# The head norm of a gated linear attention: sums by one product with a block matrix of ones, roots by logarithm and exponential on ScalarE

## The reference

```python
def rmsnorm(x, g):
    xf = x.astype(jnp.float32)
    y = xf * lax.rsqrt(jnp.mean(xf * xf, axis=-1, keepdims=True) + EPS)
    return (y * g.astype(jnp.float32)).astype(x.dtype)

    o_b, new_gla = gla_recurrence(...)          # (B, L, 4 heads, 64)
    o_b = rmsnorm(o_b.astype(x.dtype), gla_g.reshape(GLA_HEADS, GLA_DV))
    b_out = o_b.reshape(B, L, GROUP_W) * jax.nn.silu(g_z)
```

## Time and profile before

| what | value |
|---|---|
| median of 3 runs | 2264.63 us (2263.82 to 2267.15) |
| profiled execution, first to last instruction | 2263.7 us |
| PE busy | 2224.6 us, 98% |
| PEld, DVE, ACT, POOL busy | 80%, 58%, 40%, 5% |
| TensorE clock granted | 0.999 |

### The profile page before, as it was taken

How to read it: one execution, slowest core, us unless ns; L and a number is a source line. 1 busy time by engine, 2 the same in 40 slices (tenths; PEclk the granted TensorE clock), 3 DMA queues, 4 the chain that set the end, 5 groups by cost and what they waited for, 6 DMA issues and landing times.

```text
span 2263.7 us, 39453 instructions
## 1 busy us (share of the span) xinstructions
PE 2224.6 (98%) x14668; PEld 1809.6 (80%) x14668; DVE 1309.4 (58%) x2870; ACT 897.3 (40%) x2015; POOL 105.2 (5%) x179
## 2 busy tenths in 40 slices
PE   8999999999999999999999999999999999999998
PEld 4778877788788888878877878777878888887877
DVE  4467655565376755646536776556645666654542
ACT  4444233353454333434425442244435542343321
POOL 1000000000000000000000000000000000000000
PEclk9999999999999999999999999999999999999999
DMA  7111212244211122324331121232441112241332
GB/s 250 32 57 29 57 38 66 66 147 139 85 39 30 43 64 74 72 77 137 132 89 44 29 52 43 52 96 78 141 135 42 44 30 64 48 103 38 97 110 75
DMA packets 230552, 172.08 MB, mean 76 GB/s; under 512 B 56886, under 2 KB 206908, under 8 KB 230332
## 3 DMA queue, kind: packets, MB, share of 16 engines
q1 hardware_dynamic: 226100, 154.78, 24.3%
q10 hardware_dynamic: 4264, 14.78, 1.9%
HBM read 136.60 MB, written 21.93 MB: 70 GB/s over the span
## 4 chain that ended last, share of the span: by engine, by line
PE 51%; DVE 1%; issue 1%; ACT 0%; DVEq 0%; ACTq 0%; POOLq 0%; POOL 0%
PE bank L1767 27%; PE bank L2814 13%; PE bank L1861 2%; PE bank L2071 1%; PE bank L2046 1%; PE bank L2022 1%; PE bank L2830 1%; PE bank L1839 1%; PE bank L2027 1%; PE bank L1845 1%; PE bank L1910 0%; PE bank L1814 0%; PE bank L1908 0%; PE bank L1934 0%; PE bank L1911 0%
## 5 line engine op out<-in xcount | busy, mean ns | idle before, releaser
L1767 PE MATMUL bank<-h_hi,w_hi 128*128 128x512 f32 (+3 forms) x2160 | 482.9, 361 | 15.1 <-issue 5.7
L1767 PE MATMUL bank<-h_lo,w_hi 128*128 128x512 f32 (+3 forms) x2160 | 484.6, 361 | 1.7
L1767 PE MATMUL bank<-h_hi,w_lo 128*128 128x512 f32 (+2 forms) x2080 | 462.5, 360 | 2.2
L1767 PEld LDWEIGHTS bank<-h_hi,w_hi 128*128 128x128 f32 (+1 forms) x2160 | 353.2, 186 | 90.7 <-issue 32.7
L1767 PEld LDWEIGHTS bank<-h_lo,w_hi 128*128 128x128 f32 (+1 forms) x2160 | 352.3, 185 | 72.7 <-issue 15.1
L1767 PEld LDWEIGHTS bank<-h_hi,w_lo 128*128 128x128 f32 x2080 | 345.3, 188 | 64.7 <-issue 12.9
L2814 PE MATMUL bank<-scr_r,tb_r 128*128 128x512 f32 x816 | 195.1, 395 | 1.0 <-issue 1.0
L2814 PEld LDWEIGHTS bank<-scr_r,tb_r 128*128 128x128 f32 x816 | 151.7, 188 | 35.6 <-issue 2.3
L2139 ACT ACTIVATE tb<-bank 128x512 f32<-128x512 f32 (+1 forms) x140 | 71.5, 510 | 226.2 <-PE bank L1767 217.3
L2295 ACT ACTIVATE scr<-bank 128x1024 f32<-128x1024 f32 x64 | 65.8, 1027 | 194.9 <-PE bank L2046 194.9
L2814 PE MATMUL bank<-w_hi,tb_r 128*128 128x512 f32 x544 | 136.1, 394 | 0.0
(11 more groups left out here) (299 smaller groups left out, 2928.1 us busy)
## 6 DMA issues: line engine op xcount, KB each, us to landing
w_raw<-in_w_in SPq DMA_DIRECT2D x96, 512.0 KB, 3.8
out<-scr SPq DMA_DIRECT2D x32, 512.0 KB, 2.7
scr<-in_w_out SPq DMA_DIRECT2D x16, 512.0 KB, 5.3
w_raw<-in_w_out SPq DMA_DIRECT2D x16, 512.0 KB, 3.6
scr<-in_x_prompt SPq DMA_DIRECT2D x16, 512.0 KB, 3.7
scr<-out SPq DMA_DIRECT2D x16, 512.0 KB, 3.4
rot<-out ACTq DMA_DIRECT2D x12, 512.0 KB, 3.7
mix_t<-in_x_prompt ACTq DMA_DIRECT2D x8, 512.0 KB, 14.9
```

The source lines that it names most:

```text
L1767: m = mm(bank[b][0:m_w, 0:c1 - c0], w[:, slot, k, 0:m_w], h[:, k, c0:c1], start=it["piece"] == 0 and k == 0, stop=it["piece"] == 2 and k = ...
```

## The change

The squares now move through PE and a 128x128 block matrix of ones (`heads_one`, which has a one where row and column belong to the same head) stands as weights: one fp32 product of 128x512 puts the sum of each head on all 64 partitions of that head. So nothing has to be spread or turned. ACT takes the logarithm of the sum / 64 + EPS straight from bank 7, frees the bank, and takes exp(-0.5 x) in place; DVE multiplies from SBUF. `spread` is gone, and a part `root` on ACT (due when the sums are there) stands in its place; `gla_norm` no longer uses PE or bank 6, and POOL has no part in the norm.

```diff
@@ planner, Forecast.place
-            p = run("PE", 0.38 if small else 1.0, self.needs(it))
-            p = run("DVE", 0.2, p)
+            at[("full", n)] = run("PE", 0.14 if small else 0.86, self.needs(it))
+        elif k == "root":
+            p = self.table_run("ln", 0.25 if small else 0.65, when(("full", n)))
             self.free(p, 7)
-            at[("root", n)] = run("POOL", 0.8 if small else 1.7, p)
-        elif k == "spread":
-            at[("spread", n)] = run("DVE", 0.25 if small else 0.45, when(("root", n)))
+            at[("root", n)] = self.table_run("exp", 0.25 if small else 0.65, p)
         elif k == "gla_norm":
-            p = run("PE", 0.27 if small else 0.66, self.needs(it))
-            self.free(run("DVE", 0.3 if small else 0.78, p), 6)
-            run("DVE", 0.3 if small else 0.78)
+            run("DVE", 0.35 if small else 1.5, self.needs(it))
@@ TensorE
                     emptied(pe, it, 7)
-                    for c in range(n_ch):
-                        m = mm(bank[7][0:tw, 2 * c:2 * c + 2], sq[:, c * tw:(c + 1) * tw], heads_one[:, 0:P:HD],
-                               start=True, stop=True)
-                    m.then_inc(bank_full[7], 1)
-                elif kind == "gla_norm":
...
-                    for c in range(n_ch):
-                        m = nc.tensor.transpose(bank[6][:, c * tw:(c + 1) * tw],
-                                                qb_of(s)[0:tw, P * c:P * c + P], ident[0:tw, 0:tw])
-                    m.then_inc(bank_full[6], 1)
+                    mm(bank[7][:, 0:w], heads_one[:], sq, start=True, stop=True).then_inc(bank_full[7], 1)
@@ ScalarE
+                elif kind == "root":
...
+                    filled(act, it["of"], 7)
+                    link(fn(r, bank[7][:, 0:w], ACT.Ln, scale=1.0 / HD, bias=tiny[:]))
+                    act.drain().then_inc(bank_free[7], 1)
+                    fn(r, r, ACT.Exp, scale=-0.5).then_inc(rs_done, 1)
@@ VectorE
-                elif kind == "gla_sq":
...
-                    ts(z, bank[7][0:tw, 0:2 * n_ch], 1.0 / HD, EPS, ALU.mult, ALU.add).then_inc(ms_done, 1)
-                    dve.drain().then_inc(bank_free[7], 1)
-                elif kind == "spread":
...
-                    nc.vector.tensor_copy(qb_of(s)[0:tw].rearrange("p (x d) -> p x d", d=HD),
-                                          z.rearrange("p (x o) -> p x o", o=1).to_broadcast([tw, 2 * n_ch, HD])
-                                          ).then_inc(spread_done, 1)
                 elif kind == "gla_norm":
...
-                    filled(dve, it, 6)
-                    link(tt(r, bank[6][:, 0:w], area(lay, "o"), ALU.mult))
-                    dve.drain().then_inc(bank_free[6], 1)
+                    dve.wait_ge(rs_done, norm_no[s["n"]])
+                    link(tt(r, r, area(lay, "o"), ALU.mult))
@@ GpSimd
-                elif kind == "gla_sq":
...
-                    tt(z, z, minus_half[0:tw].to_broadcast([tw, n]), ALU.pow).then_inc(rs_done, 1)
```

More of the change, by code:

```diff
@@ L200, in needs @@
                  "gla_sq": [("sq", n), ("state", n, it.get("last", 0))],
-                 "gla_norm": [("spread", n)],
+                 "gla_norm": [("root", n)],
                  "score": [("turned", n), ("q", n), ("keyed", n), ("kct", n)],
@@ L523, in work @@
             out.append(item("gla_sq", [7], step=s, last=chunks - 1))
-            out.append(item("gla_norm", [6], step=s))
+            out.append(item("gla_norm", step=s))
         else:
@@ L597, in emit @@
         elif kind == "gla_norm":
-            while ("spread", n, 0) not in placed:
-                emit_part("spread")
+            while ("root", n, 0) not in placed:
+                emit_part("root")
         if kind == "gla_o":
@@ L623, in emit @@
         elif kind == "gla_sq":
-            parts.append((fc.at[("root", n)], "DVE", item("spread", step=it["step"], of=it)))
+            parts.append((fc.at[("full", n)], "ACT", item("root", step=it["step"], of=it)))
         elif kind == "evict" and it["role"] == "z":
@@ L736, in ready @@
         kind, n, c = it["kind"], it["step"]["n"] if "step" in it else 0, it.get("c", 0)
-        part = {"turn": ("scale", n, c), "fac_prod": ("fac_exp", n, it.get("i", 0)), "gla_norm": ("spread", n, 0)}.get(kind)
+        part = {"turn": ("scale", n, c), "fac_prod": ("fac_exp", n, it.get("i", 0)), "gla_norm": ("root", n, 0)}.get(kind)
         held = [float("inf") if behind_turn(x) else when + PART_US["held"] for when, _, x in parts if x["kind"] == "soft" and keeps_banks(x)
@@ L1162, in on_gpsimd @@
         def on_gpsimd(pool):
+            nc.gpsimd.memset(tiny[:], EPS)
             nc.gpsimd.memset(minus_half[:], -0.5).then_inc(out_sq_done, 1)
```

37 lines of the change are left out of this document (7 added, 30 removed).

## The result

The changed kernel takes 2307.61 us (median of 4 runs, 2300.63 to 2310.81) against 2264.99 of the kernel before beside it; ratio 1.0182, 95% interval 1.0165 to 1.0199. It is slower, as forecast, but by 43 us where I had written 14, and above the range of 2262 to 2297. The profiled execution is the fastest of the four: span 2298.8 us, 35.1 over the span before. Each timed run of this study lies 1.8 us above its span (2300.63 and 2298.8 here), not a tenth of a microsecond as I had concluded from the runs before; that moves the forecast by one microsecond and changes no reading.

The account below looks back on a forecast made before the run. It took the time to be the sum of what PE issues, the order hiding nearly all else. Waits grow by 30 us, PE work falls by 16: net +14 on 2263.7, so 2278 us, 8-in-10 range 2262 to 2297.

Parts of the forecast that it names:

- What PE saves: PE, norm product, transposes and turns: 12 us in prompt steps, 2 in sample steps, 2 in turns; 16 us (10 to 20).
- the turns and the sample steps: PE: fewer turns away from projections save 2 us (0 to 4), the four sample steps 2 us (0 to 3).
- Rival D: ACT's roots: no loads between Ln and Exp, so no waits at the ends of B; about 2255 us, chance 0.02.
- The block of 3.8 us: ACT, end of each B step: one root as two table loads, a logarithm and an exponential, 3.8 us together.
- Place by place: Second pass: PE waits of 2.5, 2.5, 1.5, 0.7 at B group ends, 8.6 in unit C; less today's 1.9, 13.9.
- PE's busy time: A sign of the forecast over the whole kernel: PE busy lower by some 15 us.
- place 5: Unit C, group 1, second half: no projections between, so the softmax chain sets the pace; PE waits 8.6 us (4 to 11).
- A: Rival: ACT reaches the roots earlier, waits are absorbed and grow by 6 against 16 saved; 2254 to 2255 us, chance 0.12.
- B: Rival: waits at the B ends at half, place 5 at 5.5, cancelling the saving; about 2265 us, chance 0.10.
- place 1: End of B group 0, first half, second pass: the root delays ACT's eviction, so PE waits 2.5 us.
- C: Rival: delays spread from one B end to later slots, the B-end waits doubled, place 5 at 11; 2300 us, chance 0.10.
- place 2: End of B group 0, second half, second pass: PE waits 2.5 us for ACT's work and DVE's gate after it.

Follow-up runs that it names:

- e9_idle: The kernel before with one idle pause on TensorE ahead of each of the 16 prompt steps' norm products; 2362.26 us, ratio 1.0429.
- e10_filled: The kernel before with the same 16 waits as e9_idle, filled with three products whose results are thrown away; 2327.62 us, ratio 1.0275.
- e11_short: The kernel before with the pauses of e9_idle at half the length (GpSimd operation 128x6 in place of 128x16); 2313.41 us, ratio 1.0211.
- e2_noload: The changed kernel with Tanh in place of the logarithm, same order, 40 table loads fewer; 2293.93 us, ratio 1.0132.
- e3_oldorder: The changed kernel's operations with the planner's costs of the kernel before, so nearly the old order; 2275.81 us, ratio 1.0056.
- e12_rest: The changed kernel with one planner constant changed (REST_US 2.0 to 0.0), giving another order in the C slot; 2281.19 us, ratio 1.0061.
- e6_replanned: The changed kernel with all its loads under other planner costs, the root due 2 us after its product; 2256.76 us, ratio 0.9968.
- e16_e7noload: The change with Tanh for Ln in the control's order, a 128x8 product standing where the four transposes stood; 2250.84 us, ratio 0.9942.
- the control: The kernel before, without the change, under retuned planner constants (EARLY 0.4, REST_US and RETURN_US 0, soft 4.5); 2251.87 us, ratio 0.9940.

## Why the prediction was wrong in size

**The step that failed** is the sentence that the clock plays no part because it is granted in full in the kernel before. That was true of a kernel with hardly any wait over 1.3 us, and I then forecast some sixteen waits of 1 to 4.4 us and priced them at their length alone. In the profiled run the lower level cost up to 21 us more than before, in the median run about 30, where the forecast had nothing. e9_idle and e10_filled show the mechanism, e11_short that it reaches down to waits of 1.5 us in about half of the cases. With the price of e9_idle (2.3 for 3.1) on the forecast's waits of 2 us and more, 2.5 + 2.5 + 4.4 + 2.0 in each second pass, 2 x 11.4 x 0.74 = 17 more, the forecast would have been 2295, inside my range and still 13 under the median.

**What PE saves.** Forecast 16 us, measured 13.4. The new product costs 0.86 us in place of the 0.95 that I took, the lower bound: 0.46 from its start to the next projection, and the one behind that comes 0.40 late. Twenty of them:

```profile
L1926 PE MATMUL bank<-scr,heads_one 128*128 128x512 f32 x16 | 8.2, 592 | 0.0
L1926 PE MATMUL bank<-mix_t,heads_one 128*128 128x512 f32 x16 | 8.2, 591 | 0.0
...
L1926 PE MATMUL bank<-scr,heads_one 128*128 128x64 f32 x8 | 1.3, 245 | 0.0
```

So the 16 prompt steps gave 16 x (1.70 - 0.86) = 13.4 instead of 12. The whole rest of the span fell by no more than that, so the turns and the sample steps together gave nothing that this split shows, where I had put 4 on them.

**The loads.** 81 in the program where there were 41; the 40 more stand one ahead of each of the root's two activations:

```profile
L2218 ACT ACT_TABLE_LOAD x20 | 25.7, 1283 | 0.5
L2220 ACT ACT_TABLE_LOAD x20 | 25.7, 1283 | 2.1
```

Rival D is out. The block of 3.8 us is 3.9.

**The waits.** Forecast +30, measured +27.4. Place by place in the first of the second passes: 2.5, 2.5, 1.5, 0.7 and 8.6 were forecast, 2.3, 3.0, 1.8, none and 8.7 measured (0.7 of the last was there before). Each first pass has one of 2.1 where I had said 1; e2_noload keeps it, so the loads are not its cause. PE's busy time, which I expected to fall by 15, rose by 7, since products at half clock count longer: as a sign it needs the clock beside it. What I put down to order (place 5) was order: e3_oldorder, e12_rest and e6_replanned don't have it (the waits of the transposes are none over 0.7, 0.5 and at most 1.4 us there).

**The rivals.** A and B ask for smaller waits than the trace has: 2.33 us at place 1, where A has none, and 8.7 in the C slot, where A has 4 and B 5.5. C gave 2300 through delays that spread; the trace shows no such spread, its waits over 1 us are those of the places and those that the kernel before had, but for the one in each first pass, and it was near by its number only. None of the cases had the clock in it, and the range's upper end, half way to C, was therefore worked out from waits alone.

**Still open.** e16_e7noload has no added load and is only 1 us faster than the control. By the split its rest is 9.4 us less; 2.7 more of idle time, among it a wait of 1.1 us for DVE's gate at place 2 of each second pass, and up to 4.9 more of the clock take most of it back. Of its five stretches at half level three stand behind the sample step's small products, as the control's two do, and one ahead of the first pass, where the change has no part. So the activations of 128x512 on ScalarE, or the norm that comes later, cost a few microseconds at most; which of the two, no run here tells apart. What the new operations would take in this order without the stand-in wasn't run; its 0.49 us in 20 places is some 10 us, an estimate from the rows above, which would leave the kernel with the real root near 2272 us, still over the control's 2251.9. Open too is why the small products of the sample step bring a stretch in 16 of 24 cases and not in the others.

## What to carry to other kernels

When TensorE is busy 98% of the time, price a wait that you add at more than its length: here a pause of 3.1 us cost 5.4, and products without use in its place, 3.9 us for each pause, kept the clock up. Compare span times granted clock beside span, before and after; what only the span shows is the clock's, what both show is work and waits. When you put a small instruction in as a stand-in, price it too: a 128x8 product cost 0.49 us among projections. Where a planner or scheduler sets the order, run the old operations under a retuned order too before you credit the new ones: here the retuned kernel before (2251.9) beats the retuned changed one (2256.8), and both beat what they came from.

## What the runs showed of the hardware that I had not expected

- The granted clock falls at waits of 1.5 to 1.7 us in 7 of 16 cases (e11_short) and at waits of 3.1 us in 16 of 16 (e9_idle), in a PE stream that is otherwise full; it stays down for 3.4 or 6.8 us, in the C slot of the changed kernel, where more waits follow, for 10.2 and 17.1.
- It also falls where PE has no idle time: in 16 of 24 places where 24 small products, 16 of them of 128x8, stand together with no projection between, and in none of 40 where projections stand ahead and behind the sixteen.
- The same program on the same data has different stretches from run to run and between its two layers: the four runs of the changed kernel lie 10 us apart with clocks of 0.988 to 0.984, those of the kernel before 3.3 apart.
